# Expert weights loaded by half matrices in order of use, a new order of blocks on VectorE, and empty slots left out of gather and scatter

## The reference

```python
y = hier_moe(x1, ...)         # top-1 group of 4, then top-2 of its 8 experts
    # each expert's tokens are padded to blocks of MOE_BLOCK = 128 slots
    xb = xt[slot_tok].reshape(NB, MOE_BLOCK, D)
    def run_block(args):
        xblk, e = args
        h = jax.nn.silu(xblk @ w_gate[e]) * (xblk @ w_up[e])   # (1024, 512) each
        return h @ w_down[e]                                   # (512, 1024)
    y = segment_sum(yb * slot_w, slot_tok)
ple = (p[i] @ w_ple[i]) * sigmoid(x1 @ w_ple_gate[i] + ple_gate_b[i])
x = layer_norm(alpha * x1 + y + ple)
```

## Time and profile before

| | |
|---|---|
| three runs | 2064.98, 2067.24, 2072.45 us; median 2067.24 |
| profiled execution, span from first to last instruction | 2062.2 us |
| TensorE busy, VectorE, ScalarE, GpSimd | 1806.4, 1059.5, 826.6, 304.1 us |
| mean granted TensorE clock | 0.932 |
| expert matrices loaded | 32 of each kind, 2048 KB each |
| gathers and scatters of 128 rows | 32 of each |

### The profile page before, as it was taken

How to read it: one execution, slowest core, us unless ns; L and a number is a source line. 1 busy time by engine, 2 the same in 40 slices (tenths; PEclk the granted TensorE clock), 3 DMA queues, 4 the chain that set the end, 5 groups by cost and what they waited for, 6 DMA issues and landing times.

```text
span 2062.2 us, 27399 instructions
## 1 busy us (share of the span) xinstructions
PE 1806.4 (88%) x8478; PEld 1452.6 (70%) x8478; DVE 1059.5 (51%) x1307; ACT 826.6 (40%) x1077; POOL 304.1 (15%) x335
## 2 busy tenths in 40 slices
PE   7999999999988898989897898789888899899830
PEld 6888888888865586868676676677677677677720
DVE  2015655500125544243446634776776776777737
ACT  3132233211234313131213213666766766767621
POOL 0112212110100010000000120012221222111217
PEclk9999999999977898999999999899999999999965
DMA  6242333222423234242224266678878878888663
GB/s 233 87 118 106 121 115 114 98 78 92 150 98 116 94 114 142 92 158 92 87 104 136 81 209 250 269 314 342 358 305 349 348 309 362 329 333 360 263 239 128
DMA packets 100534, 396.62 MB, mean 192 GB/s; under 512 B 17921, under 2 KB 25345, under 8 KB 88194
## 3 DMA queue, kind: packets, MB, share of 16 engines
q1 hardware_dynamic: 77778, 319.45, 41.0%
q0 software_dynamic: 22704, 76.49, 9.8%
HBM read 331.01 MB, written 64.94 MB: 192 GB/s over the span
## 4 chain that ended last, share of the span: by engine, by line
PE 64%; DMA 9%; ACT 8%; DVE 8%; issue 6%; POOL 2%; ACTq 1%; SPq 0%; DVEq 0%; POOLq 0%
PE ps L796 42%; PE ps L1072 11%; DMA arena<-in_expert_w_up 6%; ACT act_h L1131 5%; PE ps L1088 2%; DVE act_l L1811 2%; PE ps L963 2%; PE ps L877 1%; PE ps L904 1%; ACT arena L1131 1%; PE ps L1039 1%; ACT blk_h L1131 1%; POOL arena L769 1%; DVE wgt_l L1452 1%; DVE blk_l L1818 1%
## 5 line engine op out<-in xcount | busy, mean ns | idle before, releaser
L1811 DVE TENSOR_TENSOR act_l<-arena,act_h 128x1024 fp32r<-128x1024 f32 x256 | 296.4, 1217 | 150.3 <-ACT act_h L1131 149.9
L1131 ACT ACTIVATE act_h<-arena 128x1024 fp32r (+2 forms) x280 | 266.9, 1025 | 159.6 <-DMA arena<-in_expert_w_up 146.1
L796 PE MATMUL ps<-act_h,wgt_h 128*128 128x512 f32 x768 | 304.7, 397 | 16.2 <-DVE act_l L1622 7.2
L796 PE MATMUL ps<-act_l,wgt_h 128*128 128x512 f32 x768 | 301.9, 393 | 0.0
L796 PE MATMUL ps<-act_h,wgt_l 128*128 128x512 f32 x768 | 301.4, 392 | 0.0
L1131 ACT ACTIVATE wgt_h<-arena 128x1024 fp32r (+3 forms) x220 | 222.8, 1032 | 188.8 <-PE ps L796 66.9
L1131 ACT ACTIVATE arena<-ps 128x512 f32<-128x512 f32 (+5 forms) x245 | 143.7, 605 | 354.9 <-PE ps L796 298.1
L796 PE MATMUL ps<-wgt_h,act_h 128*128 128x512 f32 (+1 forms) x640 | 249.6, 390 | 12.5 <-DVE act_l L1626 4.6
L1452 DVE TENSOR_TENSOR wgt_l<-arena,wgt_h 128x1024 fp32r<-128x1024 f32 (+2 forms) x92 | 102.7, 1144 | 293.5 <-ACT wgt_h L1131 289.1
L1131 ACT ACTIVATE arena<-arena 128x512 f32<-128x512 f32 (+4 forms) x131 | 82.1, 642 | 410.3 <-DVE arena L1494 121.3
L796 PE MATMUL ps<-wgt_l,act_h 128*128 128x512 f32 (+1 forms) x640 | 244.1, 381 | 0.0
(11 more groups left out here) (166 smaller groups left out, 2548.1 us busy)
## 6 DMA issues: line engine op xcount, KB each, us to landing
arena<-in_expert_w_gate SPq DMA_DIRECT2D x32, 2048.0 KB
arena<-in_expert_w_up SPq DMA_DIRECT2D x32, 2048.0 KB, 8.9
arena<-in_expert_w_down SPq DMA_DIRECT2D x32, 2048.0 KB, 13.1
arena<-in_w_in SPq DMA_DIRECT2D x13, 2048.0 KB, 9.6
z_t<-arena POOLq DMA_DIRECT2D x56, 256.0 KB, 2.3
arena<-z_t SPq DMA_DIRECT2D x40, 256.0 KB, 2.8
arena<-y_n SPq DMA_DIRECT2D x16, 512.0 KB, 5.4
kv_n<-arena POOLq DMA_DIRECT2D x24, 256.0 KB, 2.3
```

What stands on the lines that cost most here:

```text
L796: ins = pe.matmul(out, left(x, k), right(y, k), start=k == 0 and (x, y) == (0, 0), stop=k == KC - 1 and x == 1)
L1131: return act.activation(out, in_, f, **kw)
L1811: dve.tensor_tensor(dst[:, w * c:w * (c + 1), :], arrived(src, m, b, slice(w * c, w * (c + 1))), f(high[:, w * c:w * (c + 1), :]), ALU.sub ...
```

## The change

Three parts. (a) The ring is filled in the order gate(b+1), up(b+1), down(b), with slot numbers to match (`ring_slot`), in halves with a semaphore each: gate(b) follows up(b-2), up(b) follows down(b-3), down(b) follows gate(b), each half after the two quarters lying there have been lowered. The loads before the loop are reordered, and ScalarE waits by halves. (b) In `block_step` hidden(b) comes after three of the four low quarters of up(b+1), and step 0 has the order of the others; ScalarE's step 0 too. (c) Empty slots get a token number of at least SEQ, which the gather's bounds test drops, and the scatter drops rows from 2 x SEQ on; xb is filled with zeros once. The five engines' tick semaphores, which nothing waits for, become one.

```diff
+        slot_e = take(MAXB, dt=I32)
-        m_ld, m_hi, m_lo, m_used = sems("moe_ld", 3), ...
+        m_ld = [sems(f"moe_ld{m}_", 2) for m in range(3)]
+        m_hi, m_lo, m_used = ...
+        slot_ok = sem("slots_marked")
-        t_sp, t_act, t_pe, t_dve, t_pool = (sem(f"tick_{n}") for n in ("sp", "act", "pe", "dve", "pool"))
+        t_sp = t_act = t_pe = t_dve = t_pool = sem("tick")
+        def ring_slot(m, b):
+            if isinstance(b, int) and b == 0:
+                return (0, 1, 4)[m]
+            return (b * 3 + (-1, 0, 4)[m]) % RING
...
-            def load_weight(b, m, e, started):
...
+            def load_half(b, m, h, e):
+                if not (isinstance(b, int) and b == 0):
+                    sp.wait_ge(m_ld[m][h], b * 16)
                     sp.sem_inc(t_sp, 1)
...
+                n = SLOT // 2
+                src = (a["expert_w_gate"], a["expert_w_up"], a["expert_w_down"])[m][0, bass.ds(e, 1)].rearrange(
+                    "e (p k) n -> p e (k n)", p=P)[:, :, h * n:(h + 1) * n]
+                dst = ring.rearrange("p (r n) -> p r n", r=RING)[:, bass.ds(ring_slot(m, b), 1), h * n:(h + 1) * n]
+                sp.dma_start(dst, src).then_inc(m_ld[m][h], 16)
+            def lowered(m, count):
+                sp.wait_ge(m_lo[m], count)
+                sp.sem_inc(t_sp, 1)
@@ in the PG stage, pieces t = 3, 4, 5 of its second half
-                        load_weight(0, t - 3, e_first, False)
+                        # t == 3: gate(0), both halves; t == 4: up(0)
+                        # t == 5, after lg_tp and x1_stored: gate(1)
@@ after it
-            for m in range(3):
-                load_weight(1, m, e_next, False)
-            with sp.Fori(2, n_blocks) as b:
-                e_next = expert(b)
-                for m in range(3):
-                    load_weight(b, m, e_next, True)
+            for j in range(2):
+                sp.wait_ge(pp_done[j], NT)
+            for h in range(2):
+                load_half(1, 1, h, expert(1))
+            for j in range(2):
+                sp.wait_ge(z2_st[j], 16 * NT)
+            for h in range(2):
+                load_half(0, 2, h, expert(0))
+            e_next = expert(2)
+            for m in range(2):
+                for h in range(2):
+                    lowered(m, WC // 2 * (h + 1))
+                    load_half(2, m, h, e_next)
+            e_down = expert(1)
+            for h in range(2):
+                lowered(0, WC + WC // 2 * (h + 1))
+                load_half(1, 2, h, e_down)
+            with sp.Fori(3, n_blocks) as b:
+                e_next = expert(b)
+                for h in range(2):
+                    lowered(1, b * WC + (WC // 2 * (h + 1) - 2 * WC))
+                    load_half(b, 0, h, e_next)
+                for h in range(2):
+                    lowered(2, b * WC + (WC // 2 * (h + 1) - 3 * WC))
+                    load_half(b, 1, h, e_next)
+                e_down = expert(b + -1)
+                for h in range(2):
+                    lowered(0, b * WC + (WC // 2 * (h + 1) - WC))
+                    load_half(b + -1, 2, h, e_down)
@@ gpsimd
+                                        bounds_check=SEQ - 1, oob_is_err=False).then_inc(xb_ld, 16)
...
+            pool.tensor_scalar(slot_e, slots[:, :, 1], float(2 * SEQ), float(SEQ), ALU.is_ge, ALU.mult).then_inc(slot_ok, 1)
+            pool.wait_ge(slot_ok, 1)
+            pool.tensor_tensor(slots[:, :, 0], slots[:, :, 0], slot_e, ALU.add).then_inc(slot_ok, 1)
+            pool.memset(xb, 0.0).then_inc(slot_ok, 1)
+            pool.wait_ge(slot_ok, 3)
             gather(0, 0)
...
+                                        bounds_check=2 * SEQ - 1, oob_is_err=False).then_inc(y_st, 16)
@@ scalar
             def split_expert(m, b, dst, src, done, free):
-                act.wait_ge(m_ld[m], b * 16 + 16)
-                act.sem_inc(t_act, 1)
                 for c in range(WC):
+                    if c % 2 == 0:
+                        act.wait_ge(m_ld[m][c // 2], b * 16 + 16)
+                        act.sem_inc(t_act, 1)
...
             def step(b, first, last):
-                if not last and not first:
+                if not last:
                     split_expert(0, b + 1, wgt_h, ring_up, gm_done, True)
...
-                if first:
-                    split_expert(2, 0, d_h, ring_down, y_done, False)
-                    split_expert(0, 1, wgt_h, ring_up, gm_done, True)
                 if not last:
                     split_expert(1, b + 1, u_h, ring_up, um_done, True)
                     x_high(b + 1, True)
+                split_expert(2, b, d_h, ring_down, y_done, not first)
                 if not first:
-                    split_expert(2, b, d_h, ring_down, y_done, True)
                     y_out(b - 1)
@@ vector
             def block_step(b, first, last):
-                if first:
-                    hidden(b, True)
-                    low_expert(2, b, d_l, d_h, ring_down)
                 if not last:
                     low_expert(0, b + 1, wgt_l, wgt_h, ring_up)
-                    low_expert(1, b + 1, u_l, u_h, ring_up)
-                if not first:
-                    hidden(b, False)
+                    low_expert(1, b + 1, u_l, u_h, ring_up, range(WC - 1))
+                hidden(b, first)
                 if not last:
+                    low_expert(1, b + 1, u_l, u_h, ring_up, range(WC - 1, WC))
                     x_low(b + 1)
-                if not first:
-                    low_expert(2, b, d_l, d_h, ring_down)
+                low_expert(2, b, d_l, d_h, ring_down)
```

More of the change, by code:

```diff
@@ L319, in build @@
         z2_st = sems("z2_st", 2)
-        m_ld, m_hi, m_lo, m_used = sems("moe_ld", 3), sems("moe_hi", 3), sems("moe_lo", 3), sems("moe_used", 3)
+        m_ld = [sems(f"moe_ld{m}_", 2) for m in range(3)]
+        m_hi, m_lo, m_used = sems("moe_hi", 3), sems("moe_lo", 3), sems("moe_used", 3)
+        slot_ok = sem("slots_marked")
         idx_ok, xb_ld, xt_done, xt_hi, xt_lo = (
@@ L528, in expert @@
                 return sp.value_load(be_row[0:1, bass.ds(b, 1)], min_val=0, max_val=NE - 1)
-            def load_weight(b, m, e, started):
-                w = (a["expert_w_gate"], a["expert_w_up"], a["expert_w_down"])[m]
-                if started:
-                    sp.wait_ge(m_lo[(m + 1) % 3], (b + (m == 2) + -1) * WC)
+            def load_half(b, m, h, e):
+                if not (isinstance(b, int) and b == 0):
+                    sp.wait_ge(m_ld[m][h], b * 16)
                     sp.sem_inc(t_sp, 1)
[L539 to L560, removed]
+                n = SLOT // 2
[6 more added lines that the diff above has]
+                sp.sem_inc(t_sp, 1)
             def store_z2(i, t):
@@ L578, in _ @@
                     if i == 1 and 3 <= t < 6:
-                        load_weight(0, t - 3, e_first, False)
+                        if t == 3:
+                            sp.wait_ge(w_lo, WC * S_END)
+                            for h in range(2):
+                                load_half(0, 0, h, e_first)
+                        if t == 4:
+                            for h in range(2):
+                                load_half(0, 1, h, e_first)
+                        if t == 5:
+                            sp.wait_ge(lg_tp, 1)
+                            for j in range(2):
+                                sp.wait_ge(x1_stored[j], 16 * (NT // 2))
+                            e_second = expert(1)
+                            for h in range(2):
+                                load_half(1, 0, h, e_second)
                 if i == 0:
@@ L586, in _ @@
             n_blocks = sp.snap(sp.value_load(nb_i[0:1, 0:1], min_val=0, max_val=MAXB - MINB) + MINB)
-            e_next = expert(1)
-            for m in range(3):
-                load_weight(1, m, e_next, False)
-            with sp.Fori(2, n_blocks) as b:
-                e_next = expert(b)
-                for m in range(3):
-                    load_weight(b, m, e_next, True)
+            for j in range(2):
+                sp.wait_ge(pp_done[j], NT)
+            for h in range(2):
+                load_half(1, 1, h, expert(1))
+            for j in range(2):
+                sp.wait_ge(z2_st[j], 16 * NT)
[11 more added lines that the diff above has]
+            with sp.Fori(3, n_blocks) as b:
+                e_next = expert(b)
+                for h in range(2):
+                    lowered(1, b * WC + (WC // 2 * (h + 1) - 2 * WC))
+                    load_half(b, 0, h, e_next)
+                for h in range(2):
+                    lowered(2, b * WC + (WC // 2 * (h + 1) - 3 * WC))
+                    load_half(b, 1, h, e_next)
+                e_down = expert(b + -1)
+                for h in range(2):
+                    lowered(0, b * WC + (WC // 2 * (h + 1) - WC))
+                    load_half(b + -1, 2, h, e_down)
+            b_last = sp.snap(n_blocks + -1)
+            e_down = expert(b_last)
+            for h in range(2):
```

(15 more changed lines are left out.)

2 lines of the change are left out of this document (1 added, 1 removed).

## The result

| | before | changed |
|---|---|---|
| median (lowest, highest) of four runs | 2067.01 (2064.98, 2072.45) | 1943.90 (1940.55, 1946.22) |
| ratio | 1 | 0.9402, 95% interval 0.9387 to 0.9417 |
| span of the profiled execution | 2062.2 | 1944.3 |

Faster by 123.1 us; 1945 was forecast. The profiled execution is the slowest of the changed kernel's four (1946.22 us), so its span is the yardstick for rows and the medians for the whole.

What follows compares the result with a forecast made beforehand. Bound: the up matrix's load latency inside each expert step, making TensorE wait. 111.7 us from 29 steps plus 11.0 from step 0 make 122.7, taking 2067.2 to 1945 us; range 1932 to 1955 (chance 0.57), 8 in 10 up to 1988.

Steps and rivals of the forecast that it cites:

- The wait: Expert steps: ScalarE waits 5.0 us a step for the up matrix, whose load is tied to the step before's end.
- The price of a step: Expert loop: 17.9 us a step instead of 21.75, over 29 steps, 111.7 us saved.
- four parts: TensorE's step: gate and up matmuls 10.91 us, token transposes 0.91, down matmuls 5.48, hidden transposes 0.47.
- The clock: TensorE in expert steps: idling lowers its granted clock to a mean of 0.95; it should come near 1.0.
- Step 0: First expert step: reordered VectorE and ScalarE work lets step 1 start about 1290.2, 11.0 us gained.
- rival 1: Expert steps: DMA engines become the bound, 18.1 us at the poorer rate (16.1 at the better); mostly 1956 to 1991; chance 0.25.
- My sign for this rival: Expert steps: DMA-bound loads would show as ScalarE waiting for whichever matrix is next and a DMA share at 1.0.
- Halves at nothing: Weight loads: half matrices cost nothing between issues, and their earlier start is worth nothing given 23 us of slack.
- Rows at nothing: Gather and scatter: fewer rows only shorten a transfer loop that already has 3.3 us of slack; taken as 0.
- Marking slots at nothing: Before the first gather: two small GpSimd operations and a fill, over 45 us of cover; cost 0, uncovered up to 5.
- rival 3: Scatter: bounds test and bookkeeping add over 7.2 us to a 128-row transfer; 10 us added gives 2139; chance 0.03.
- the 5.0 us carried over from span to median: Whole kernel: median 2067.24 lay 5.0 us above the profiled span 2062.2; the forecast kept that difference.

Runs made afterwards that it cites:

- b1: Kernel before with the new ring order alone (whole matrices, old blocks, all rows): ratio 0.9450, steps of 17.85 us.
- a1: Changed kernel with every row gathered and scattered again, order, halves and blocks kept: ratio 0.9403, steps of 17.86 us.
- a2: Changed kernel with each matrix loaded whole by one 2 MB transfer instead of halves: ratio 0.9412, steps of 17.86 us.
- b4: Changed kernel plus one extra 1 MB memory-to-memory copy a step: ratio 0.9636, steps of 19.69 us.
- c2: Changed kernel plus the extra 1 MB copy a step, and all rows gathered and scattered again: ratio 0.9668, steps of 19.81 us.
- b2: Kernel before with empty rows left out of gather and scatter, and the shared tick semaphore: ratio 0.9941, steps of 21.20 us.
- c1: Kernel before with half-matrix loads in its own ring order, nothing else: ratio 0.9662, steps of 19.48 us.

## Why the prediction was right

**The wait.** Right, and shown by b1: the load's latency was in the loop because of the order, and the order alone takes it out.

**The price of a step.** Forecast 17.9, measured 17.76, so every one of the four parts stood at its best value: 10.91, 0.90, 5.48, 0.47. I had added 0.14 for quarters held by each other; there are none. 630.62 - 515.04 = 115.6 us for the forecast 111.7.

**The clock** needed no term of its own: with TensorE never idle the 12.75 us matmuls of the earlier trace rows are all 10.91. It did shape the start: step 0's took 14.06, step 1's 12.75.

**Step 0.** Forecast 11.0 us, measured 9.7, since its matmuls took 14.06 us for 13.25; the layout of ScalarE and VectorE held, with step 1 starting 5.7 us after the end of up(0), where 5.2 was forecast. Step 1 gave 1.1 that I had not counted: I had let it keep its 13.84 us of matmuls, and they took 12.75. In a1 and a2 they took 14.01 and 13.90 and step 0 was 19.1 us, so some of this is spread; steps 0 and 1 together take 39.4 us here and 39.9 there.

**The DMA engines** (rival 1). It didn't decide, but the argument that put it aside was weaker than it looked. Both times that I weighed, 16.1 and 18.1 us, took the dropped rows as relief, and b4 with c2 says that they are almost none. By the 7.34 MB figure I had kept for that case, 17.4 us, the bound is 0.4 us under TensorE's; by the sum over the loaded half it is 0.6 under. My sign for this rival, a share of 1.0, was wrong as a sign: the share was 1.0 without it. The right ones are ScalarE's waits for loads and a step that grows with bytes on the loaded engines.

**Halves at nothing:** right in the new order (a2), by the reason given. The 19.9 and 20.0 us a step, for half loads that each pay for themselves, didn't come: queued behind each other they moved 386 GB/s here and 425 in c2. **Rows at nothing:** right (a1). **Marking slots at nothing:** right; timeline of GpSimd in the changed kernel:

```profile
1219.87 0.40 POOL L774 TENSOR_SCALAR arena<-arena 128x48 int32<-128x48 int32 x1 [5.92 <-DMA arena<-slot_tok]
1220.35 0.28 POOL L776 TENSOR_TENSOR arena<-arena 128x48 int32<-128x48 int32 x1
1220.58 0.95 POOL L777 MEMSET arena<- 128x1024 f32 x1
```

1.6 us in front of a gather whose tokens are split at 1275.83. **The bounds test** (rival 3) costs nothing that shows. The fair pairs differ in the rows alone: the scatter instruction takes 1.02 us at the median in the changed kernel and 0.99 in a1, 2.68 in b2 and 2.72 before. That it is so much shorter in the new order, and lands 8.0 us after issue instead of 12.6, comes with the new queue, since a1 has it too (8.4), and not with the rows.

**Coming within 1.1 us** was luck. The named pieces of the two profiles gave 126.3 us, 3.6 more than the 122.7 forecast. And the 5.0 us carried over from span to median are no fixed difference: the changed kernel's median lies 0.4 us under its span. The spread between executions, 8.3 us ahead of step 0 alone, made up for both. What holds without luck is the step, 17.76 us for 17.9.

## What to carry to other kernels

Lay out a ring in the order of use, and check for each load which event frees its slot and how long before the use that is; a load tied to the end of the step before has its latency in the loop however deep the ring is. Several parts that cure one wait don't add up, and once the wait is gone each is worth what it does elsewhere (here step 0), so undo them one by one and run each alone as well. Parts that act in different places do add. Price the bound that lies behind the wait first: it sized this gain to 4 us of 116.

## What the runs showed of the hardware

- A row dropped by the bounds test still makes a packet, of 4 bytes instead of 4 KB and 9 ns instead of 159 (from 1350 to 1800 us, 3,909 packets of 4 bytes and 3,325 of 4 KB on this queue; in a1 816 and 6,528). The page's table of queues, changed kernel; before, the same queue had as many packets with 76.49 MB:

```profile
q0 software_dynamic: 22704, 59.73, 8.4%
```

- The DMA share reads 1.00 at 384 GB/s and 1.01 at 405, 416 and 425 GB/s. The highest rate sustained over 450 us was 425 GB/s.
- When empty slots are left out, about half of the engines' shares of a gather or scatter hold no row at all and a third keep all eight (103 and 79 of 218 in b4): the relief goes to one part of the engines, and the other sets the pace.
- VectorE's scalar_tensor_tensor and GpSimd's two-input operations were held up by each other, even at one column (2.28 us for 0.16); VectorE's tensor_scalar, reciprocal and statistics ran beside GpSimd at their own 0.15 to 0.71 us. Only the last pass of this kernel shows it.
- The scatter's median landing was 12.6 us before, 10.9 in b1 and 11.0 in a2 (new order, whole matrices), 10.3 in c1 (old order, halves), and 8.4 in a1 and 8.0 in the changed kernel (both). Order and halves each take some 2 us off, the dropped rows next to nothing. That a row passes sooner between packets of 8 KB than of 16 KB is my reading of the halves' part; no run shows the cause.
